# Recurrent block's output product: three output tiles channel block by channel block, then the fourth; two of the ten low parts made by VectorE

## What is computed

```python
def rglru_mixer(h, w_in, conv_w, conv_b, w_a, b_a, w_i, b_i, lam, w_out, h0_f, h0_b):
    gate_br, x_br = jnp.split(h @ w_in, 2, axis=-1)
    xc = centred_dwconv(x_br, conv_w, conv_b)
    y_f, s_f = rglru_scan(xc, w_a[0], b_a[0], w_i[0], b_i[0], lam[0], h0_f, False)
    y_b, s_b = rglru_scan(xc, w_a[1], b_a[1], w_i[1], b_i[1], lam[1], h0_b, True)
    y = (y_f + y_b).astype(h.dtype) * jax.nn.gelu(gate_br)
    return y @ w_out, jnp.stack([s_f, s_b], axis=1)
...
        xp = xp + mod_p[:, :, 5] * yp
        xs = xs + mod_s[:, :, 5] * ys
```

## Time and profile before

| | |
|---|---|
| median of 3 runs | 1561.41 us (1561.37 to 1562.25) |
| the profiled execution's own time | 1562.63 us |
| its span (first to last instruction) | 1561.0 us |
| PE matmuls busy | 1515.5 us, 97% of the span |
| mean granted TensorE clock | 0.992 of full speed |
| output stage of the recurrent block, first to last matmul | 448.16 to 492.4 us |

### The profile page before, as it was taken

The page is one execution under the profiler, slowest core; times in us unless marked ns, Lnnn a source line. Parts: engine busy times, 40 slices in busy tenths (PEclk is TensorE's granted clock), DMA queues, the critical chain, the costliest instruction groups (busy, mean ns, idle before and its releaser), DMA issues.

```text
span 1561.0 us, 24626 instructions
## 1 busy us (share of the span) xinstructions
PE 1515.5 (97%) x8780; PEld 1476.5 (95%) x8780; DVE 1129.1 (72%) x1717; ACT 661.2 (42%) x956; POOL 185.7 (12%) x279
## 2 busy tenths in 40 slices
PE   7999999999979999999999999999889999999998
PEld 4799999999979999999999999998779999999998
DVE  5798888888987877788887777986977574444432
ACT  4333342259975433332343333225545454333321
POOL 0010000100250000001000000100795000000000
PEclk9999999999989999999999999999999999999999
DMA  9366676623423555577545556753222134334421
GB/s 382 143 249 225 210 249 221 220 75 108 145 86 125 199 188 192 195 229 235 186 162 189 190 186 228 241 193 113 79 71 86 62 109 142 126 123 142 153 93 41
DMA packets 68280, 257.04 MB, mean 165 GB/s; under 512 B 7585, under 2 KB 8609, under 8 KB 67969
## 3 DMA queue, kind: packets, MB, share of 16 engines
q1 hardware_dynamic: 48944, 187.57, 35.2%
q0 software_dynamic: 18512, 67.58, 12.8%
q10 hardware_dynamic: 768, 1.19, 0.2%
HBM read 253.68 MB, written 2.63 MB: 164 GB/s over the span
## 4 chain that ended last, share of the span: by engine, by line
PE 88%; DVE 4%; ACT 3%; POOL 2%; issue 1%; DMA 0%; DVEq 0%; SPq 0%; ACTq 0%; POOLq 0%
PE bank L557 25%; PE bank L559 25%; PE bank L558 25%; PE bank L656 2%; PE bank L570 1%; ACT w_hi_sb L1006 1%; PE bank L626 1%; PE bank L623 1%; PE bank L622 1%; PE wide L859 1%; DVE w_lo_sb L1479 1%; DMA ada_first<-in_ada_w 0%; PE bank L881 0%; DVE bcum L2050 0%; DVE h_lo L1586 0%
## 5 line engine op out<-in xcount | busy, mean ns | idle before, releaser
L1006 ACT ACTIVATE w_hi_sb<-raw 128x1024 fp32r<-128x1024 f32 (+3 forms) x308 | 344.1, 1122 | 477.2 <-PE bank L559 455.1
L557 PE MATMUL bank<-h_hi,w_hi_sb 128*128 128x384 f32 x1567 | 529.1, 338 | 2.3 <-ACT vt L1449 1.0
L1479 DVE TENSOR_TENSOR w_lo_sb<-raw,w_hi_sb 128x1024 fp32r<-128x1024 f32 (+3 forms) x308 | 403.4, 1311 | 172.5 <-ACT w_hi_sb L1006 169.5
L559 PE MATMUL bank<-h_hi,w_lo_sb 128*128 128x384 f32 x1567 | 526.6, 336 | 0.0
L558 PE MATMUL bank<-h_lo,w_hi_sb 128*128 128x384 f32 x1567 | 526.6, 336 | 0.0
L557 PEld LDWEIGHTS bank<-h_hi,w_hi_sb 128*128 128x128 f32 x1567 | 294.6, 188 | 6.5 <-DVE h_lo L1586 2.1
L558 PEld LDWEIGHTS bank<-h_lo,w_hi_sb 128*128 128x128 f32 x1567 | 294.7, 188 | 0.0
L559 PEld LDWEIGHTS bank<-h_hi,w_lo_sb 128*128 128x128 f32 x1567 | 294.6, 188 | 0.0
L557 PE MATMUL bank<-a_hi,w_hi_sb 128*128 128x384 f32 x704 | 236.9, 336 | 1.5 <-DVE a_lo L1701 1.5
L559 PE MATMUL bank<-a_hi,w_lo_sb 128*128 128x384 f32 x704 | 236.6, 336 | 0.0
L558 PE MATMUL bank<-a_lo,w_hi_sb 128*128 128x384 f32 x704 | 236.5, 336 | 0.0
(11 more groups left out here) (312 smaller groups left out, 1636.5 us busy)
## 6 DMA issues: line engine op xcount, KB each, us to landing
raw<-in_ffn_in SPq DMA_DIRECT2D x176, 512.0 KB, 3.6
ada_raw<-in_ada_w POOLq DMA_DIRECT2D x128, 512.0 KB, 3.6
raw<-in_ffn_out SPq DMA_DIRECT2D x64, 704.0 KB, 4.5
raw<-in_rg_in SPq DMA_DIRECT2D x20, 512.0 KB, 3.6
ada_first<-in_ada_w SPq DMA_DIRECT2D x8, 1024.0 KB, 18.0
raw<-in_rg_out SPq DMA_DIRECT2D x8, 640.0 KB, 3.8
raw<-in_gla_qk SPq DMA_DIRECT2D x8, 512.0 KB, 4.0
raw<-in_gla_v SPq DMA_DIRECT2D x8, 512.0 KB, 3.4
```

The lines of the kernel that those rows point to most:

```text
L557: pe.matmul(out, w_hi_sb[:, slot, w], hi[k], start=start and j == 0, stop=False)
L559: last = pe.matmul(out, w_lo_sb[:, slot, w], hi[k], start=False, stop=stop and j == len(ks) - 1)
L1006: A(w_hi_sb[:, s, 0:w], raw[:, s, 0:w], ACT.Copy).then_inc(w_hi, 1)
L1479: V.tensor_tensor(w_lo_sb[:, s, 0:w], raw[:, s, 0:w], w_hi_sb[:, s, 0:w].bitcast(F32), ALU.subtract).then_inc(w_split, 1)
```

## The change

Three edits:

- PE. `arriving` is no longer called for this stage. For k = 0 to 7 three tiles (banks 4 to 6) are worked on together, 9 matmuls per k; the wait for the split of a weight block now stands before the first matmul that reads it, so the fourth block's is not waited for here. After k = 7 the fourth tile (bank 7) does its k = 0 to 7 in one row, 24 matmuls. Then PE waits for a new semaphore `rg_ylast` to reach 2, and finishes all four tiles with k = 8 and 9 as before. The number of matmuls is the same.
- POOL. `low_y(8)` and `low_y(9)` after its loop are gone.
- DVE. After `outputs(9)` it makes the low parts 8 and 9 itself, each after a wait for the high part, and counts `rg_ylast`.

```diff
@@ -526,8 +527,6 @@
                         if m >= 2:
                             low_y(m - 2)
-                    for m in (RC - 2, RC - 1):
-                        low_y(m)
@@ -774,7 +773,22 @@
             pe.wait_ge(gate_read, 4 * RC)
             pe.wait_ge(rg_p, RC)
-            arriving(base, range(RC), y_chunks, rg_yhi, rg_yready, 0, RC - 2, bank[4:8])
+            for k in range(RC - 2):
+                w = slice(k * P, (k + 1) * P)
+                pe.wait_ge(rg_yhi, k + 1)
+                for b in range(RING - 1):
+                    if k == 0:
+                        pe.wait_ge(w_split, base + b + 1)
+                    pe.matmul(bank[4 + b][:, 0:T], w_hi_sb[:, b, w], y_chunks[0][k], start=k == 0, stop=False)
+                    pe.matmul(bank[4 + b][:, 0:T], w_lo_sb[:, b, w], y_chunks[0][k], start=False, stop=False)
+                pe.wait_ge(rg_yready, k + 1)
+                for b in range(RING - 1):
+                    pe.matmul(bank[4 + b][:, 0:T], w_hi_sb[:, b, w], y_chunks[1][k], start=False, stop=False)
+            pe.wait_ge(w_split, base + RING)
+            tile(bank[7][:, 0:T], RING - 1, range(RC - 2), *y_chunks, True, False)
+            pe.wait_ge(rg_ylast, 2)
+            for b in range(RING):
+                tile(bank[4 + b][:, 0:T], b, range(RC - 2, RC), *y_chunks, False, True, RC - 2).then_inc(w_used, 1)
@@ -2003,6 +2017,10 @@
             outputs(9)
+            for m in (RC - 2, RC - 1):
+                dve.wait_ge(rg_yhi, m + 1)
+                V.tensor_tensor(y_lo[:, m, :], y32[:, m, :], y_hi[:, m, :].bitcast(F32),
+                                ALU.subtract).then_inc(rg_ylast, 1)
             V.sem_inc(drained, len(RG_SEQ))
             mixer_out("rg_out", 0, 1, 2, [4, 5, 6, 7, 0, 1, 2, 3])
```

More of the change, by code:

```diff
@@ L315, in build @@
         rg_yready = sem("rg_yready")
+        rg_ylast = sem("rg_ylast")
         rgc_ready = sem("rgc_ready")
```

## The result

| | before | changed |
|---|---|---|
| median of 7 runs | 1561.81 us (1560.61 to 1565.87) | 1566.15 us (1564.42 to 1569.84) |
| profiled execution, its own time | 1562.63 us | 1564.90 us |
| its span | 1561.0 us | 1563.2 us |

The changed kernel takes 1.0027 times as long, 95% interval 1.0017 to 1.0038: +4.2 us, between +2.7 and +5.9. Beside later experiments, on another occasion, it took 1.0024 (1.0014 to 1.0034). The forecast was +3.6 us.

The account below looks back on a forecast made before the run. PE's row of matmuls was taken as the bound. Work left behind the eighth low part (+2.4 us) plus the clock's fall (+1.2) gave +3.6 us on the median 1561.41: 1565.0 us, range 1563.3 to 1566.8.

Parts of the forecast that it names:

- The bound: Whole kernel: PE is busy 97% of the span and holds 88% of the chain; only breaks in its matmul row matter.
- Part 1, the start: Start of the output stage: without waiting for the fourth weight block's split, PE starts at about 445.4, 2.8 us sooner.
- Part 2, the loop: Joint loop, 9 matmuls per k: PE outruns its inputs from k = 5, with holes at k = 6 and 7; early start used up.
- the second case that the text names: Joint loop, k = 5: if the clock returns sooner, PE waits for the high part and is still done at 457.7.
- my 2.9: Joint loop, k = 6: PE idle for 2.9 us until POOL's low part comes at 462.15.
- Part 3, 51 matmuls behind low part 7: After the eighth low part: 51 matmuls, 8.85 us, remain; four tiles end at 473.85 instead of 471.45, +2.4 us.
- Part 4, DVE's two low parts: Low parts 8 and 9 on DVE: ready between 466.3 and 467.0, asked for at 469.7, so hidden with 2.7 us to spare.
- Part 5, nothing given back: Behind the four tiles: later tiles, x, norm and loads all move by the same amount and give nothing back.
- Part 6, the clock: Holes between 459.25 and 463.59: PE's clock likely falls to its lower level, costing 0.65 to 1.56 us or more, taken as 1.2.
- The case that it holds: Rival, PE's clock stays full through the loop's holes: +2.4 us, 1563.8 us; chance 0.38.
- the early start carrying through: Rival, output stage: parts of y come in time, PE does 120 matmuls in one row, 2.55 us sooner, 1558.9 us; chance 0.03.
- a single fall: Main case, holes of the joint loop: PE's clock falls for one stretch, 1564.5 to 1565.3 us; chance 0.47.

Follow-up runs that it names:

- e5: Changed kernel plus throw-away 128 x 128 matmuls in the two holes, before low part 6 and high part 7: 1563.85 us, 1.0018 of the kernel before.
- e3: Changed kernel with two tiles instead of three in the joint loop, the other two doing their 24 matmuls each afterwards: 1570.05 us, 1.0056 of the kernel before.
- e1: Changed kernel with low parts 8 and 9 given back to POOL: 1565.62 us, 1.0022 of the kernel before.
- e2: Kernel before, old four-tile order kept, but low parts 8 and 9 made by DVE: 1561.81 us, 0.9998 of the kernel before.
- e4: Changed kernel with POOL making low part 6 ahead of copying block 8's state: 1566.09 us, 1.0023 of the kernel before.
- e6: Against the kernel before: three tiles for k = 0 and 1, fourth catches up, then four together; POOL keeps low parts 8, 9: 1562.62 us, 1.0001.
- e8: Three tiles, fourth catches up at k = 2, DVE's low parts, high-part matmuls of k = 8, 9 first: 0.9993 and 0.9994 of the kernel before.

## Why the prediction was right, point by point

**The bound.** PE's unbroken row decides, and what matters is where it is broken. Right.

**Part 1, the start.** 445.4 was said, 0.2 us after the last read of the gates; it was 0.05 after it (444.05 against 444.00). Right.

**Part 2, the loop.** The clock came back sooner than I had assumed (from 447.1 the matmuls are 0.29 and then 0.17 us apart, while in the profile of before it came back at 451.2), so PE was ahead at k = 5 already and waited there 1.10 us, the second case that the text names. The hole at k = 6 was 2.62 us by the row; counted as my 2.9 was, from the start of the sixth matmul plus 0.17, it is 461.03 - 458.24 = 2.79. The hole of 0.9 us at k = 7 all but vanished (0.11 us): the clock had fallen before it, and k = 6's last matmuls filled it at half speed. The wait at k = 5 shows that the early start is used up there.

**Part 3, 51 matmuls behind low part 7.** The term that decides. 8.85 us was said for them; from 464.49 to 473.33 (the last starts at 473.16, and one takes 0.17) it is 8.84. With the clock held the stage grew by 2.40 (e5), and +2.4 was the sum. e3 gives the same rule at another dose.

**Part 4, DVE's two low parts.** Both at 465.23, asked for at 469.17: hidden by 3.9 us where 2.7 was said, the rest being the clock's fall on PE and subtractions at the short end of the range. The late end of that range, 467.0, was summed wrongly: two subtractions of 1.19 one after the other from 465.26 end at 467.6, with 2.1 us to spare. Either is enough. e1 shows that they bring nothing in the new order, and e2 that they would have brought 0.64 us in the old one.

**Part 5, nothing given back.** The fifth tile starts 0.09 us after the fourth ends in the changed kernel, 0.08 before. The spans of the profiled executions differ by 2.2 us, with 1.2 us gained ahead of the stage and 3.1 lost in it, so 0.3 us came on top later. The second profile of the changed kernel arrives at the stage like the kernel before (445.18), loses 3.08 in it and has a span 3.3 us longer, again some 0.3 on top. Over all the profiles what follows the stage differs from before by -0.9 to +0.3 us, so the 0.3 says nothing, and that nothing is given back is shown to within about a microsecond.

**Part 6, the clock.** The fall was rightly taken as the likelier: it is in both profiles of the changed kernel and in those of e1, e3 and e4. The case that it holds did not come true. By the rule of the Trainium skill ("TensorE: Matmul & The Clock Gate", section "HAM oscillation — how this bites in real kernels") only a longer idle gap brings the lower clock back; here it came at the end of a hole of 2.62 us, and where the page and the trace differ the trace decides. The size was off: this is the term that was mis-sized. I took 1.2 us, and it was 0.7 in both profiles of the changed kernel (29.42 and 29.39 against the 28.71 of e5), close to the lower bound of 0.65, since the stretch lay on the holes and on k = 7's matmuls with the high part, not on the 51. Against the same 28.71 it was 1.1 in e1 and 2.3 in e4. What it cost in the executions that were not profiled is unknown.

**The number.** +3.6 us was forecast; measured were +4.2 (2.7 to 5.9) and, once more, +3.7 (2.2 to 5.3), and 3.1 in the trace of the stage. The median of 1566.15 lies within the range, 1563.3 to 1566.8, but above the 1564.5 to 1565.3 that were given to a single fall, which is what both profiles show; the second median, 1565.34, is at the edge of it. The rivals: with the early start carrying through the kernel would have been faster, and e6 shows that this start is worth nothing even where it loses nothing. What stays open is the 1.1 us between the stage's +3.1 and the ratio's +4.2 (0.6 in the second measurement): it is inside the interval, and no run here separates it from chance. So the mechanism and the +2.4 were right, while that +3.6 lies so near to +3.7 and +4.2 is in part luck, since 1.2 was taken for a term that the profiles put at 0.7. The sum also gave the lower clock on the last gates as the reason why the profiled execution of before was 1.2 us over its median. That is not borne out: the first profile of the changed kernel has the lower clock there too and arrives 1.22 us sooner.

## What to carry to other kernels

Where an engine consumes parts as they arrive, count the work that is left behind the last part that binds; that count times the pace is the cost, and work done earlier is free only while the consumer would otherwise wait. An early start is worth nothing if the consumer runs dry later. Work that is put off to pay for it costs its full length while the same part binds (23 matmuls more behind low part 7 in e3, 4.1 us); where another part came to bind, the difference of the two arrivals came off (27 matmuls more in the changed kernel, 4.7 us, but low part 7 comes 2.3 us sooner than low part 9 did: 2.4 us). So keep all the accumulators in the joint loop, let the late one catch up, and leave only what truly needs the last part behind it (e8, a stage 1.24 us shorter than before). A hole on TensorE can cost twice, since the clock may fall in it and the work behind pays (0.71 us here, e5).

## What the runs showed of the hardware that was not expected

At the end of a hole of 2.62 us the lower clock came in both profiles of the changed kernel; filling most of it with throw-away 128 x 128 matmuls kept full clock (e5). In e1 the three matmuls after a hole of 2.61 us still ran at full clock, and those after the next hole, of 0.64 us, did not. And closing one hole does not help when the wait only moves: in the profile of e4 one hole of 3.42 us instead of one of 2.62 and a short second one was followed by a low stretch twice as long, with 16 matmuls at 0.32 us instead of nine, and the stage was 1.6 us longer although PE had its input 2.8 us sooner. That is one execution; the median time of e4 does not show it, and whether the longer hole is the cause is open.
